# A two-layer decoder trunk: first weights in four pieces, heads' halves on ScalarE and VectorE, another state-space layout

## What is computed

```
h = rms_norm(x, mix_norm);  proj = h @ w_in                 # 768 | 256 columns
state[t] = lam_bar * state[t-1] + b_bar @ u[t]              # 48 groups, complex
y = real(c @ state) + d_skip * u;  g = gelu(y);  main = g * sigmoid(g @ w_glu + b_glu)
x = x + concat(main, memory_attention(q)) @ w_out;  x = x + swiglu(rms_norm(x))
x = x + concat(causal(q, K, V), memory_attention(q)) @ w_out1
x = x + sum over the top 2 experts of gate_e * swiglu_e(rms_norm(x))
```

## Time and profile before

| | us |
|---|---|
| median of three runs | 1474.73 |
| the profiled execution | 1474.49, span 1472.8 |
| TensorE busy in the span | 1439.1 (98%) |
| VectorE, ScalarE, GpSimd busy | 1191.7, 978.0, 100.2 |
| on the chain that ended last | PE 91%, ACT 2%, POOL, DVE, DMA and queues 1% each |
| of it the three-pass products, L425 | 78% |
| up to the first expert's product | about 470 |

### The profile page before, as it was taken

How to read it: one execution, slowest core, us unless ns; L and a number is a source line. 1 busy time by engine, 2 the same in 40 slices (tenths; PEclk the granted TensorE clock), 3 DMA queues, 4 the chain that set the end, 5 groups by cost and what they waited for, 6 DMA issues and landing times.

```text
span 1472.8 us, 20745 instructions
## 1 busy us (share of the span) xinstructions
PE 1439.1 (98%) x7832; PEld 1209.2 (82%) x7832; DVE 1191.7 (81%) x1190; ACT 978.0 (66%) x954; POOL 100.2 (7%) x130
## 2 busy tenths in 40 slices
PE   8989999999989999999999999999999999999997
PEld 4678799998869888888888888888888888888886
DVE  6895455555777988988898898888889889888887
ACT  5326444444674777877777777787787777778775
POOL 1753100000240000000000000000000000000000
PEclk9999999999999999999999999999999999999999
DMA  8437655443326999999999999999999999999992
GB/s 230 145 71 260 236 192 185 147 155 115 121 109 233 349 370 371 331 362 375 337 351 360 348 357 366 378 323 363 373 337 358 366 343 349 370 373 331 359 376 94
DMA packets 193088, 425.95 MB, mean 289 GB/s; under 512 B 14002, under 2 KB 23088, under 8 KB 192944
## 3 DMA queue, kind: packets, MB, share of 16 engines
q1 hardware_dynamic: 192480, 424.35, 80.3%
q10 hardware_dynamic: 560, 0.94, 0.3%
HBM read 421.67 MB, written 1.05 MB: 287 GB/s over the span
## 4 chain that ended last, share of the span: by engine, by line
PE 91%; ACT 2%; POOL 1%; DVE 1%; issue 1%; ACTq 1%; DMA 1%; SPq 1%; DVEq 0%
PE bank L425 78%; PE bank L447 3%; PE bank L908 2%; PE bank L490 2%; PE bank L920 1%; PE bank L700 1%; PE bank L529 1%; PE bank L453 1%; ACTq L1021 1%; SPq L1081 1%; POOL work L1171 1%; ACT w_hi L1531 1%; DMA ring<-work 1%; PE bank L626 1%; DVE ring L1697 0%
## 5 line engine op out<-in xcount | busy, mean ns | idle before, releaser
L2015 DVE TENSOR_TENSOR w_lo<-ring,w_hi 128x2048 fp32r<-128x2048 f32 x341 | 777.7, 2290 | 99.6 <-ACT w_hi L1531 98.2
L1531 ACT ACTIVATE w_hi<-ring 128x2048 fp32r<-128x2048 f32 x341 | 649.1, 1917 | 129.1 <-PE bank L425 126.1
L425 PE MATMUL bank<-w_hi,xg_hl 128*128 128x512 f32 x1792 | 557.1, 392 | 0.0
L425 PEld LDWEIGHTS bank<-w_hi,xg_hl 128*128 128x128 f32 x1792 | 332.8, 188 | 67.2
L425 PE MATMUL bank<-w_lo,xg_hl 128*128 128x512 f32 x896 | 349.4, 390 | 0.0
L425 PE MATMUL bank<-w_hi,at_hl 128*128 128x512 f32 x896 | 277.5, 391 | 0.0
L425 PEld LDWEIGHTS bank<-w_lo,xg_hl 128*128 128x128 f32 x896 | 168.2, 188 | 35.8
L425 PEld LDWEIGHTS bank<-w_hi,at_hl 128*128 128x128 f32 x896 | 167.1, 188 | 33.9
L425 PE MATMUL bank<-w_lo,at_hl 128*128 128x512 f32 x448 | 174.5, 389 | 0.0
L1888 DVE TENSOR_TENSOR fpart_hl<-ring,fpart_hl 128x1024 fp32r<-128x1024 f32 x66 | 80.6, 1224 | 75.1 <-ACT fpart_hl L1439 74.9
L425 PE MATMUL bank<-ht_hl,fpart_hl 128*128 128x256 f32 x1056 | 128.0, 283 | 0.0
(11 more groups left out here) (253 smaller groups left out, 1151.7 us busy)
## 6 DMA issues: line engine op xcount, KB each, us to landing
ring<-in_l_moe_w_gate SPq DMA_DIRECT2D x58, 2048.0 KB, 8.0
ring<-in_l_moe_w_up SPq DMA_DIRECT2D x57, 2048.0 KB, 7.9
ring<-in_l_moe_w_down SPq DMA_DIRECT2D x56, 2048.0 KB, 7.9
ring<-in_l_ffn_w_gate SPq DMA_DIRECT2D x5, 2048.0 KB, 9.0
ring<-in_l_ffn_w_up SPq DMA_DIRECT2D x5, 2048.0 KB, 7.9
ring<-in_l_ffn_w_down SPq DMA_DIRECT2D x5, 2048.0 KB, 7.5
ring<-in_l_w_in SPq DMA_DIRECT2D x4, 2048.0 KB, 9.3
ring<-in_l_w_out SPq DMA_DIRECT2D x4, 2048.0 KB, 8.7
```

Source lines behind the costliest of these rows:

```text
L425: last = mm(p, lhsT=xs[a], rhs=ws[b], start=start and q == 0, stop=stop and q == 2, **kw)
L1531: ac(w_hi(n), at(e_slot(q) * SLOT + j * HALF, HALF), ACT.Copy).then_inc(S("hi"), 1)
L2015: tt(LO[e_slot(q)][:, j * HALF:(j + 1) * HALF], at(e_slot(q) * SLOT + j * HALF, HALF), w_hi(n).bitcast(fp), ALU.subtract).then_inc(S("lo"), 1)
```

## The change

- `win0a` comes in four transfers of 512 KB with semaphores of their own, issued by SyncE ahead of its loop; the product waits for the piece of its k. The 12 idle products ahead of it go; those ahead of the positions become 5, ahead of the gather 3.
- `Tm` moves to where `Wt` lay, `Kst`, `Ysb` and `Xbd` to offset 18432. The skip term is added in PSUM by TensorE (identity times `MD`), and K's groups wait for CA one by one. GpSimd clears only half of `Tm`; ScalarE clears the other half ahead of V's eviction and `Xbd` in two parts (after V, after q's eviction). `toeplitz` waits for K's eviction instead of GpSimd's addition.
- Chunks lie as 4 x 8 instead of 8 x 4 (`Ug`, `XB`, the GELU's read), so that the 8 blocks of one scan step are neighbours; the copies to `Xbd` become two for each of their four parts, on VectorE as on ScalarE. The powers are made before V is awaited. q's squares move behind mk0's, and in GpSimd's list q's root behind mk0's.
- Y's product takes the part with CA first, then the Tm part.
- O's high half is made by ScalarE from PSUM (`o_hi`), the rest by VectorE from PSUM (`o_lo`), which gives the bank back; `o_halves` and `o_out` go. `wout1b`'s parts are converted before the loop over pairs.

```
-        Tm = at(18432, 2, STEPS * PAIRS * GDIM)
+        Tm = at(B0, 2, STEPS * PAIRS * GDIM)
...
-        Kst = at(B0, STEPS, PAIRS, GDIM, rows=32)
+        Kst = at(18432, STEPS, PAIRS, GDIM, rows=32)
...
-        Ysb = at(B0, STEPS, PAIRS * GDIM, rows=64)
-        Xbd = at(B0 + 3072, 2, PAIRS, 64)
+        Ysb = at(18432, STEPS, PAIRS * GDIM, rows=64)
+        Xbd = at(18432 + 3072, 2, PAIRS, 64)
...
-        stream = [("win0a", cols("l0_w_in", 0, 512)), ("win0b", cols("l0_w_in", 512, 512)),
+        stream = [("win0a", []), ("win0b", cols("l0_w_in", 512, 512)),
...
+                            pe.wait_ge(S(f"ld_{name}{k // 2}"), 16)
...
-            idle_products(5, 12)
...
-            pe.wait_ge(S("s5_ca"), 12)
+            pe.wait_ge(S("skip"), 1)
             for ri in range(2):
                 read_out(pe, ("cT", ri))
             kb = [unit(pe, ("K", n), 4 + n) for n in range(2)]
             for jq in range(6):
                 c0 = jq % 4 * P
+                pe.wait_ge(S("s5_ca"), 2 * jq + 2)
                 for ri in range(2):
                     for a in range(4):
                         mm(kb[jq // 4][32 * a:32 * a + 32, c0:c0 + GDIM], lhsT=W0bd[:, ri, jq * 4 + a], rhs=cT[:, ri, jq * 4 + a],
-                           start=(jq % 4 == 0 and ri == 0), stop=(ri == 1), skip_group_check=True)
+                           start=(jq % 4 == 0 and ri == 0), stop=False, skip_group_check=True)
+                for a in range(4):
+                    mm(kb[jq // 4][32 * a:32 * a + 32, c0:c0 + GDIM], lhsT=ident[0:32, 0:32], rhs=MD[:, jq * 4 + a],
+                       start=False, stop=True, skip_group_check=True)
...
+            yb = [unit(pe, ("Y", n), n) for n in range(3)]
+            pe.wait_ge(S("xbd"), 12)
+            for n in range(3):
+                for a in range(4):
+                    for ri in range(2):
+                        for jh in range(2):
+                            j = 8 * n + 4 * jh + a
+                            mm(yb[n][64 * jh:64 * jh + 64, a * P:(a + 1) * P], lhsT=Xbd[:, ri, j], rhs=CA[:, ri, j],
+                               start=(a == 0 and ri == 0), stop=False, skip_group_check=True)
             pe.wait_ge(S("tm"), 16 * 16)
-            yb = [unit(pe, ("Y", n), n) for n in range(3)]
             for n in range(3):
                 for a in range(4):
                     for jh in range(2):
                         j = 8 * n + 4 * jh + a
                         for g2 in range(2):
                             r0 = 64 * jh + 32 * g2
-                            mm(yb[n][r0:r0 + 32, a * P:(a + 1) * P], lhsT=Ug[:, g2 * PAIRS + j], rhs=Tj[:, g2, j],
-                               start=(a == 0), stop=False, skip_group_check=True)
-            pe.wait_ge(S("xbd"), 4)
-            for n in range(3):
-                for a in range(4):
-                    for ri in range(2):
-                        for jh in range(2):
-                            j = 8 * n + 4 * jh + a
-                            last = mm(yb[n][64 * jh:64 * jh + 64, a * P:(a + 1) * P], lhsT=Xbd[:, ri, j], rhs=CA[:, ri, j],
-                                      start=False, stop=(ri == 1), skip_group_check=True)
+                            last = mm(yb[n][r0:r0 + 32, a * P:(a + 1) * P], lhsT=Ug[:, g2 * PAIRS + j], rhs=Tj[:, g2, j],
+                                      start=False, stop=True, skip_group_check=True)
                 ready(last, ("Y", n))
...
-                    pe.wait_ge(S("m0_ct"), k - 5)
+                    read_out(pe, ("m0", "O", k - 6))
...
-                pe.wait_ge(S("a1_ct"), k + 1)
+                read_out(pe, ("a1", "O", k))
...
-            idle_products(6, 8)
+            idle_products(6, 5)
...
-            idle_products(7, 7)
+            idle_products(7, 3)
...
-            eng.wait_ge(S("kst_d"), 1)
-            eng.wait_ge(S("tm_zero"), 1)
+            for n in range(2):
+                read_out(eng, ("K", n))
+            eng.wait_ge(S("tm_zero"), 2)
...
+            for q in range(4):
+                load(at(q * 1024, 2, 512), w["l0_w_in"][q * 256:(q + 1) * 256, 0:512].rearrange("(k p) n -> p k n", p=P),
+                     f"ld_win0a{q}")
...
-            got(pool, ("V", 2))
-            g.memset(Tm, 0.0).then_inc(S("tm_zero"), 1)
-            g.memset(Xbd, 0.0).then_inc(S("xbd_zero"), 1)
-            for n in range(2):
-                read_out(pool, ("K", n))
-            g.tensor_tensor(Kst[:, 0], Kst[:, 0], MD, ALU.add).then_inc(S("kst_d"), 1)
+            got(pool, ("Bm", 11))
+            g.memset(Tm[:, 1], 0.0).then_inc(S("tm_zero"), 1)
+            root("mk0", 1, hss[:, 0:8], hrs[:, 0:8], HD)
             root("q0", 1, hss[:, 16:24], hrs[:, 16:24], HD)
-            root("mk0", 1, hss[:, 0:8], hrs[:, 0:8], HD)
             root("mk1", 1, hss[:, 8:16], hrs[:, 8:16], HD)
...
-            def o_halves(tag, n, dst, k, low):
-
-                read_out(pool, (tag, "O", n))
-                link(g.tensor_copy(dst[:, k], CT[:, k]))
-                g.tensor_tensor(low[:, k], CT[:, k], dst[:, k].bitcast(fp), ALU.subtract).then_inc(S(tag + "_ct"), 1)
-
-            for n in range(2):
-                o_halves("m0", n, CTH0, 6 + n, CTL0)
+            got(pool, ("m0", "O", 1))
...
-            for n in range(8):
-                o_halves("a1", n, HTHL[:, 0], n, HTHL[:, 1])
...
+            def clear(x, n):
+
+                return ac(x.rearrange("p (a b) -> p a b", b=P), ident.unsqueeze(1).to_broadcast([P, n // P, P]), ACT.Copy, scale=0.0)
+
             for n in range(12):
                 if n % 4 == 0:
                     p = got(act, ("Ug", n // 4))
-                    free(ac(Ug[:, n * 4:n * 4 + 16], p[:, :].rearrange("p (a c) -> p a c", a=16), ACT.Copy), ("Ug", n // 4))
+                    free(ac(Ug[:, n * 4:n * 4 + 16].rearrange("p a (r b) -> p a r b", r=SL),
+                            p[:, :].rearrange("p (a b r) -> p a r b", a=16, r=SL), ACT.Copy), ("Ug", n // 4))
...
+            act.wait_ge(S("s5_w0"), 4)
+            clear(Tm[:, 0], STEPS * PAIRS * GDIM).then_inc(S("tm_zero"), 1)
...
+            def clear_carried(ri):
+                clear(Xbd[:, ri].rearrange("p j c -> p (j c)"), PAIRS * 64).then_inc(S("xbd_zero"), 1)
+
+            clear_carried(0)
...
+            clear_carried(1)
             toeplitz(act, 1)
             act.wait_ge(S("scan"), 1)
-            act.wait_ge(S("xbd_zero"), 1)
+            act.wait_ge(S("xbd_zero"), 2)
             for g2 in range(2):
-                ac(Xbd[g2 * 64:(g2 + 1) * 64, 1, :, g2 * 32 + 1:g2 * 32 + 32], VX[g2 * 64:(g2 + 1) * 64, 1, :, 0:31],
-                   ACT.Copy).then_inc(S("xbd"), 1)
+                g_ = slice(g2 * 64, (g2 + 1) * 64)
+                ac(Xbd[g_, 1, :, g2 * 32 + SB:g2 * 32 + CHUNKS], VX[g_, 1, :, 0:CHUNKS - SB], ACT.Copy).then_inc(S("xbd"), 1)
+                ac(Xbd[g_, 1, :, g2 * 32 + 1:g2 * 32 + SB], VX[g_, 1, :, CHUNKS - SB:CHUNKS - 1], ACT.Copy).then_inc(S("xbd"), 2)
+            def o_hi(tag, n, dst, heads):
+
+                p = got(act, (tag, "O", n))
+                ac(dst[:, heads[2 * n][4]], p[:, 0:T], ACT.Copy).then_inc(S(tag + "_o_hi"), 1)
...
-            for n in range(2):
-                pt_out("m0", n, PT0, lambda h: False)
+            pt_out("m0", 0, PT0, lambda h: False)
+            o_hi("m0", 0, CTH0, M0_HEADS)
+            pt_out("m0", 1, PT0, lambda h: False)
             for c in range(4):
+                if c == 2:
+                    o_hi("m0", 1, CTH0, M0_HEADS)
                 weights_hi("wout0b", "wout0", c)
...
+            weights_hi("wout1b", "wout1b", 0)
             p = got(act, "kvT")
             for i in range(2):
                 cp = ac(kTkv[half(i), i:4:2], p[half(i), :].rearrange("p (h t) -> p h t", h=2), ACT.Copy,
                         scale=gp[half(i), 2:3])
             free(cp, "kvT")
+            weights_hi("wout1b", "wout1b", 1)
             q_pairs_out(1)
             win1_out(1, 0)
+            weights_hi("wout1b", "wout1b", 2)
             ng = len(A1_HEADS) // 2
             for n in range(2):
                 softmax("a1", n, PB1, lambda h: h < 12, A1_HEADS)
+            weights_hi("wout1b", "wout1b", 3)
             win1_out(1, 1)
             for n in range(ng):
                 pt_out("a1", n, PT1, lambda h: h < 12)
                 if n == 0:
                     q_pairs_out(3)
+                o_hi("a1", n, HTHL[:, 0], A1_HEADS)
                 if n + 2 < ng:
                     softmax("a1", n + 2, PB1, lambda h: h < 12, A1_HEADS)
-                if 2 <= n < 6:
-                    weights_hi("wout1b", "wout1b", n - 2)
...
-                for q in range(4):
-                    read_out(dve, ("memT", q))
-                for h in range(2):
-                    for m in range(TM):
-                        read_out(dve, ("win0", h, m))
-                head_norm([(heads_of(HS[:, m, MAIN:D]), 4) for m in range(TM)], 8, "q0", 16, sq0, None)
...
-            for n in range(3):
```

(29 more changed lines are left out.)

13 lines of the change are left out of this document (8 added, 5 removed).

## The result

The changed kernel takes 1460.42 us (median of four runs: 1458.38, 1458.93, 1461.91, 1461.99) beside 1474.76 (four runs, 1473.92 to 1476.48): the ratio of the two series is given as 0.9899, 95% interval 0.9884 to 0.9915 (the medians divide to 0.9903, inside it). That is 14.3 us less where the forecast said 9.5. The direction was right, the size too small: the result stands at the very edge of the forecast's range, whose low end was 1460.0. The median is 0.4 us inside it; by the ratio, 0.9899 of 1474.73 is 1459.8, 0.2 us outside.

A forecast was written before the change was run, and what follows sets the result against it. TensorE, without a gap in the expert stage, was taken as the bound, so time saved ahead of it arrives: -3.5 (start's +0.4 included) - 3.5 - 1.0 - 1.5 = -9.5, from 1474.5 to 1465.0 us; range 1460.0 to 1470.5, 8 in 10.

The forecast's parts named there:

- 2(b): State-space stage, transfers into Tm: SyncE's eight start at 89.9, 1.4 earlier; ScalarE's at 92.5, 1.2 later, behind evictions and clear.
- step 4: Attention of layer 1: loop +1.0 from ScalarE's new work, wait of 1.95 at the end gone; -1.0 us together.
- Step 1: First product at the start: begins at 13.85 without filler, loses 2.0 at half clock, ends 29.8 for 29.4; +0.4 us.
- Step 2: State-space stage to the last Y: ends at 113.7 instead of 117.2, -3.5 us, the start's +0.4 included; bounds 0 and -6.
- Sub-step (c): Scan in the state-space stage: new layout saves 6.2 us; it runs from 83.3 to 101.3, where it ended at 109.1.
- Rival A: State-space scan: the layout brings nothing, so that stage gives 0 and the rest stays; -6.0, 1468.5 us; chance 0.17.
- (d): State-space stage before Y: ScalarE's transfer queue, free at 103.3, decides; copies end at 105.1, last Y at 113.7.
- Step 3: Last head pair of layer 0: TensorE's 1.97 us wait for GpSimd's halves and the half clock after it go; -3.5 us.
- Step 5: Router: shorter fillers start the gather 2.4 us earlier, 0.9 of it lost at half clock; -1.5 us.
- B: Rival: half clock wherever filler went, 0.5 more at the start, 2.6 in Y, 0.9 at the gather; 1469.0 us; chance 0.09.
- C: Rival: transfers bound the expert stage, so an earlier start only waits there; 1474.5 us; chance 0.06.
- D: Rival: the attention loop turns serial, +13.8 in place of +1.0; slower, 1477.8 us; chance 0.05.

The follow-up runs named there:

- a4_one_load: Changed kernel with the first product's weights loaded in one transfer instead of four: 1461.94 us.
- c4_both_fillers: Changed kernel with 12 pairs of idle products back ahead of the first product and the router's fillers back at 8 and 7: 1461.06 us.
- a2_filler12: Changed kernel with the filler of 12 idle products back ahead of the first product: 1460.70 us.
- c1_qnorm_back: Changed kernel with q's head norm put back between VectorE's CA products: 1463.31 us.
- d2_issue_behind: Changed kernel with ScalarE made to wait for its own clear of Xbd before issuing its Toeplitz transfers: 1464.74 us.
- b2_pool_halves: Changed kernel with all halves of O given back to VectorE's copy and GpSimd, in both layers: 1466.47 us.
- a1_again: The changed kernel run again without any edit: 1459.56 us.
- b1_old_layout: Changed kernel with the old layout of the chunks, scan elements 4 apart again: 1469.04 us, ratio 0.9961 to the kernel before.

## Why the prediction was right or wrong

The direction and most of the mechanisms were right, the size was not: 9.5 us forecast, 12.5 in the traces. The step that failed is 2(b), when ScalarE issues its transfers; the term next in size is the attention loop of step 4.

**Step 1, the first product: mechanism right.** Start 13.98 for 13.85, released by ScalarE's evictions; the split hidden, as `a4_one_load` shows. The loss at half clock is 2.3 us here and 1.4 to 2.9 in the other traces without filler, where I took 2.0; so +0.8 for +0.4. The Trainium skill ("TensorE: Matmul & The Clock Gate", the section on what's actually happening) has the lower clock as the default, which activity lifts; the traces agree: with 24 halves of filler the product took 13.90 or 13.97, without them 15.4 to 16.8. What I did not see is that the filler, at half clock itself, can hold the product up: it started at 15.46 in `c4_both_fillers` and at 14.28 in `a2_filler12`.

**Step 2, the state-space stage: the sum failed here.** Forecast -3.5, measured -6.15. Sub-step (c) was right to a tenth: 768 elements in 0.958 us, 672 in 0.859, the scan 18.1 us long; it began at 82.5, not 83.3, as V's last eviction ended at 81.9 for my 83.3. The head norm taken out was worth 2.3 (`c1_qnorm_back`) for my 1.9. The Trainium skill ("SBUF — State Buffer", the section on the DMA port swizzle) has a step of 4 fp32 free; here the measurement differs and decides: 1606 ns with the step, 958 without. Rival A is out. The step that failed is (b): "ScalarE's eight come behind two q evictions and half of Xbd, at 92.5", and with it (d), "So ScalarE's queue decides: 103.3". The issues don't come behind activations that they don't wait for: the first is at 88.9, 3.6 sooner (1.0 of it because K's evictions ended at 88.8 for my 89.8), and the queue is free at 100.1, 3.2 sooner. The last Y came 2.7 us sooner than forecast (111.0 for 113.7), 2.4 of them at the start of the product (102.74 for 105.1). With the queue where it was, my own end of the scan, 101.3, and 1.8 of copies would have given 103.1: so 2.0 are this step, and 0.4 remain for the scan's earlier end (0.7) less the copies' 2.1 for 1.8. `d2_issue_behind` puts the product at 104.7 by making the premise true. That the queue would be what TensorE waits for was half right: it is in eight of the 13 traces, but at the scan's own time, not 2 us behind it. The last 0.4 is the clock: I gave the Tm part 3.2, and at full clock it took 2.83. The result lies at the good bound of -6 ("ScalarE early"), the case that I had taken as the limit.

**Step 3, the last head pair: right**, -3.4 us for -3.5; `b2_pool_halves` gives the 3.4 back, 1.7 of it through the clock.

**Step 4, attention: -2.2 for -1.0.** The end was right (-2.3 for -2.0). The loop was to cost +1.0 and cost 0.1. The mis-sized term is what ScalarE's new work adds: I counted 8.8 for it and took off 4.2, 2.5 and 1.1 for what went and what hid it; measured, the high parts cost about 1.6 and the departed roundings had cost 1.6. I had no floor in the sum: the loop of before was already 1.6 above TensorE's own work.

**Step 5, the router: -1.0 for -1.5.** The gather started 3.0 sooner against the router's product (2.4 forecast; 0.5 of it because that product itself ran at full clock), but lost 2.0 at half clock in this execution for my 0.9; in `a1_again` it lost nothing.

**The remainder.** -9.5 should have been -12.5 in the traces. The range's low end of 1460.0 was said to use half of all good bounds, but that doesn't come out: the good bounds of steps 2 to 5 lie 2.5, 0.3, 1.5 and 0.9 below their values, together 5.2, so 1460.0 uses nearly all of them, and half would have been 1462.4. That the result stands at the edge of the range and not 2 us beyond it is owed to that slip. The scatter among executions, 4.4 us in 14, most of it the clock's by the three traces, was in no term; series of four or five have medians 2.3 us apart, more than the result lies outside the range.

**The rivals.** B (half clock everywhere) held for the start and the gather, 2.3 and 2.0 us, and not for Y; C is out, the experts' loop gave only 0.3 back; D is out, no turn of the loop was above 4.8 us. With the layout alone undone B's mechanism does appear in Y, after TensorE idled for 5.32 us.

## What to carry to other kernels

An edit has no price by itself: the shorter scan was worth nothing while transfers behind another engine's clears came last, and 8 us, nearly half of it clock, once those were gone. Before costing a change, list all that the product waits for with the time of each, not only the last. Ask too of an engine's transfers what they wait for, not what they stand behind; and where two loads share one engine under another's floor, cost them together, since either alone may look cheap.

## What was not expected of the hardware

- ScalarE issued a transfer at 88.90 us with two evictions and a clear (2.7 us of work) still ahead of it in its list; with a wait for that clear it issued at 91.81. The eight issues take 11.2 and 10.8 us.
- The same VectorE addition of 384 elements in steps of 16 bytes takes 888 ns with GpSimd silent (`b1_old_layout`) and 1129 with GpSimd at work; without the step, GpSimd silent, it takes 557.
- 24 idle half products take 2.94 us in one execution and 4.71 in another of nearly the same kernel: when the clock rises after the same beginning isn't fixed. In the twelve traces without filler the first product is 15.39 to 16.84 us long, with no other cause in the trace.
